# Attention scores of a hybrid block from split queries and keys: three products in the rounded format instead of products of unsplit fp32 tiles

## What is computed

```python
c_q = rms_norm(bcq, a_cq_g)
q_b = rms_norm((c_q @ a_wuq).reshape(B, S, 16, 128), a_qn_g)
k_b = rms_norm(bk.reshape(B, S, 4, 128), a_kn_g)
v_b = bv.reshape(B, S, 4, 128)
...
# for a block of 128 queries: the best 64 keys by an index score, then
sc = einsum('bqhgd,bqkhd->bqhgk', q_blk, k_g) * 128 ** -0.5
p = softmax(where(valid, sc, -inf))
out = einsum('bqhgk,bqkhd->bqhgd', p, v_g)
```

## Time and profile before

| | |
|---|---|
| median of 3 runs | 1538.51 us (1537.47 to 1538.88) |
| the profiled execution, its own time | 1538.53 us |
| its span (first to last instruction) | 1536.8 us |
| PE busy | 1532.3 us, 6996 matmuls |
| DVE busy | 994.8 us |
| ACT busy | 753.3 us |
| POOL busy | 356.7 us |
| granted TensorE clock | 1.0 of full speed over the span |

### The profile page before, as it was taken

How to read it: one execution, slowest core, us unless ns; L and a number is a source line. 1 busy time by engine, 2 the same in 40 slices (tenths; PEclk the granted TensorE clock), 3 DMA queues, 4 the chain that set the end, 5 groups by cost and what they waited for, 6 DMA issues and landing times.

```text
span 1536.8 us, 18847 instructions
## 1 busy us (share of the span) xinstructions
PE 1532.3 (100%) x6996; PEld 1271.5 (83%) x6996; DVE 994.8 (65%) x1537; ACT 753.3 (49%) x1006; POOL 356.7 (23%) x609
## 2 busy tenths in 40 slices
PE   9999999999999999999999999999999999999999
PEld 7888888888888888888878888888888888888887
DVE  6647555666769865576579667676456767664554
ACT  6745444587544444554554535534346444443332
POOL 9041212230230040126410354346200120200000
PEclk9999999999999999999999999999999999999999
DMA  9886778886787675558856787799875765666674
GB/s 291 283 240 193 223 211 232 212 234 192 231 244 209 195 221 162 161 185 273 246 182 188 225 244 217 227 276 260 251 245 178 255 213 192 210 198 194 194 247 156
DMA packets 206268, 337.77 MB, mean 220 GB/s; under 512 B 53050, under 2 KB 60521, under 8 KB 205921
## 3 DMA queue, kind: packets, MB, share of 16 engines
q1 hardware_dynamic: 184784, 288.66, 62.2%
q0 software_dynamic: 21344, 47.90, 10.9%
q10 hardware_dynamic: 48, 0.02, 0.0%
HBM read 312.81 MB, written 23.49 MB: 219 GB/s over the span
## 4 chain that ended last, share of the span: by engine, by line
PE 98%; DVE 1%; ACT 0%; issue 0%; DMA 0%; DVEq 0%
PE acc L1048 31%; PE acc L1051 31%; PE acc L1050 31%; PE mix L1111 1%; PE mix L1184 1%; PE mix L1104 0%; PE mix L1173 0%; PE mix L1019 0%; PE acc L1252 0%; DVE w_lo L1659 0%; PE mix L1170 0%; PE mix L1160 0%; ACT w_hi L1322 0%; PE mix L1158 0%; DMA xs<-in_x_dram 0%
## 5 line engine op out<-in xcount | busy, mean ns | idle before, releaser
L1659 DVE TENSOR_TENSOR w_lo<-w_raw,w_hi 128x1024 fp32r<-128x1024 f32 (+2 forms) x535 | 646.1, 1219 | 419.4 <-ACT w_hi L1322 416.2
L1322 ACT ACTIVATE w_hi<-w_raw 128x1024 fp32r<-128x1024 f32 (+2 forms) x535 | 556.2, 1050 | 526.5 <-PE acc L1051 460.1
L1048 PE MATMUL acc<-w_hi,op_hi 128*128 128x512 f32 (+1 forms) x2036 | 799.8, 393 | 0.3 <-DVE w_lo L1659 0.3
L1051 PE MATMUL acc<-w_hi,op_lo 128*128 128x512 f32 (+1 forms) x2036 | 792.5, 389 | 0.0
L1050 PE MATMUL acc<-w_lo,op_hi 128*128 128x512 f32 (+1 forms) x2036 | 792.2, 389 | 0.0
L1048 PEld LDWEIGHTS acc<-w_hi,op_hi 128*128 128x128 f32 x2036 | 382.4, 188 | 80.1 <-issue 1.3
L1051 PEld LDWEIGHTS acc<-w_hi,op_lo 128*128 128x128 f32 x2036 | 382.1, 188 | 79.9
L1050 PEld LDWEIGHTS acc<-w_lo,op_hi 128*128 128x128 f32 x2036 | 382.4, 188 | 77.8
L792 POOL DMA_DIRECT2D conv_dram<-y x48 | 30.6, 690 | 168.6 <-ACT y L1374 167.8
L792 POOL DMA_DIRECT2D y_dram<-y x32 | 20.5, 711 | 184.2 <-DVE y L2098 114.9
L946 POOL DMA_DIRECT2D bp_dram<-b_ps x48 | 31.4, 716 | 66.9 <-ACT b_ps L1543 62.8
(11 more groups left out here) (348 smaller groups left out, 974.3 us busy)
## 6 DMA issues: line engine op xcount, KB each, us to landing
w_raw<-in_w_in_dram SPq DMA_DIRECT2D x367, 512.0 KB, 4.5
w_raw<-in_w_out_dram SPq DMA_DIRECT2D x128, 512.0 KB, 4.4
w_raw<-in_w_in_dram SPq DMA_DIRECT2D x16, 384.0 KB, 3.3
w_raw<-in_a_wuq_dram SPq DMA_DIRECT2D x12, 512.0 KB, 5.9
conv_dram<-y POOLq DMA_DIRECT2D x48, 64.0 KB, 3.8
y<-conv_dram POOLq DMA_DIRECT2D x48, 64.0 KB, 4.5
w_raw<-in_a_wuqi_dram SPq DMA_DIRECT2D x6, 512.0 KB, 4.6
bp_dram<-b_ps POOLq DMA_DIRECT2D x48, 64.0 KB, 4.0
```

The costliest lines, as they stand in the source:

```text
L1048: nc.tensor.matmul(o, hi[:, kt, tok], hv[:, i, n0:n1], start=(kt == (kts if late else blk["kts"])[0]), stop=False)
L1051: last_mm = nc.tensor.matmul(o, lo[:, kt, tok], hv[:, i, n0:n1], start=False, stop=(kt == blk["kts"][-1]))
L1322: func(split_ap(w_hi, c), w_raw[:, c % RAW_BUFS, 0:n], ACT.Copy).then_inc(hi_ready, 1)
L1659: vec.tensor_tensor(split_ap(w_lo, c), w_raw[:, c % RAW_BUFS, 0:n], split_ap(w_hi, c).bitcast(F32), ALU.subtract).then_inc(lo_ready, 1)
```

## The change

The scores are no longer products of two fp32 tiles. Queries and keys are split like the big operands: ACT rounds the transposed queries to `q_hi` (two copies of 128x512 in a new piece `bqt` on ACT) and the scaled keys to `k_hi` (the second scaling writes `k_hi` instead of `b_kT`). DVE subtracts: new pieces `bql` (two subtractions of 128x512, which write `q_lo` over `b_qT`) right behind `bqt` in the same slot, and once `bkl` (128x1024, `k_lo` over `b_kT`) three slots behind `bkt`. PE makes three fp32r matmuls for each former one: `q_hi` with `k_hi`, `q_hi` with `k_lo`, `q_lo` with `k_hi`, of the same 128 or 256 columns. PE waits in `bs` for `q_lo_ready` instead of `bq_turned`. `q_hi` lies where the raw keys lay in `kv`, `k_hi` where `lane_u` lies. To have semaphores left, the ten that told of blocks brought back (`conv_moved`, `cq_moved`, `bi_moved`, `bq_moved`, `aqk_moved`) become one pair `brought`, with the counts added up in `wait_brought`; the places that wait and signal stay the same.

```diff
@@ -197,6 +197,7 @@
     at = weave(at + 9, [("bt", 0), ("bt", 1)] + [None] * 4 + [("bt", 2), ("bt", 3)])
     assert at <= end("silu", W_A + 512 * 3) + 1, (at, end("silu", W_A + 512 * 3))
     weave(at + 5, [("bkt", 0), ("yd", 12), ("yd", 13)], 2)
+    weave(at + 8, [("bkl", 0)])
     weave(end("bi", 0) + 3, [("yd", 14), ("yd", 15)], 2)
     at = weave(end("bi", 0) + 8, [("bit", 0)] + bsc_pairs(0))
     at = weave(max(at, end("bi", 1) + 10), [("bit", 1)] + bsc_pairs(1))
...
@@ -208,7 +209,7 @@
         at = end("bq", g) + (9, 2, 3, 3)[g]
         weave(at, [("bqn", g)])
         at = max(at + 9, score + 15)
-        weave(at, [("bqt", g)])
+        weave(at, [("bqt", g), ("bql", g)])
         score = at + 2
         for v in range(3):
             weave(score + 4 * v, [("bs", (g, v))])
...
@@ -285,6 +286,7 @@
         _, csq_hi, _, csq_lo = region([("y_0", [P, W_A + 1024], F32), ("csq_hi", [P, 2, 512], F32R),
                                        ("y_1", [P, D - 1024], F32), ("csq_lo", [P, 2, 512], F32R)])
         y = sb("y", [P, M, D])
+        q_hi_0, _, q_hi_1 = region([("q_hi_0", [P, 512], F32R), ("kv_0", [P, 512], F32), ("q_hi_1", [P, 512], F32R)])
         kv = sb("kv", [P, M, 1024])
         ident = sb("ident", [P, P])
         ones = sb("ones", [P, P], F32R)
...
@@ -295,6 +297,7 @@
         par = sb("par", [P, R_N + N_TAP])
         small = sb("small", [P, M, G_W])
         align(512)
+        k_hi, = region([("k_hi", [P, HKV, SEQ], F32R)])
         lane_u, lane_t = region([("lane_u", [P, BLK, LANE_C], F32), ("lane_t", [P, 320], F32)])
         rows = sb("rows", [8, 6, SEQ])
         gcol = sb("gcol", [P, 9, 8])
...
@@ -361,6 +364,9 @@
              ("b_sq", [P, 1024], F32), ("b_qT", [P, 4, SEQ], F32), ("b_kT", [P, HKV, SEQ], F32),
              ("sc", [P, 3 * P], F32), ("b_s", [P, 512], F32), ("b_ps", [P, 2, 512], F32),
              ("b_pT", [P, 2, 4, P], F32), ("top8", [P, 8], F32)])
+        _, q_lo, k_lo = region([("b_0", [P, 2 * QKT * SEQ + M * 512 + 1024], F32), ("q_lo", [P, 4, SEQ], F32R),
+                                ("k_lo", [P, HKV, SEQ], F32R)])
+        q_hi = [v[:].rearrange("p (h t) -> p h t", h=2) for v in (q_hi_0, q_hi_1)]
         b_p = b_ps[:, 0]
         bi_in = [qs[:], b_sq[:].rearrange("p (m c) -> p m c", m=M)]
         bi_T = [v.rearrange("p q (k t) -> p (q k) t", k=2) for v in bi_in]
...
@@ -455,24 +461,23 @@
-        cq_moved = [sem(f"cq_moved{i}") for i in range(2)]
+        bk_hi_ready = sem("bk_hi_ready")
+        q_hi_ready = sem("q_hi_ready")
+        q_lo_ready = sem("q_lo_ready")
-        bi_moved = [sem(f"bi_moved{i}") for i in range(2)]
-        bq_moved = [sem(f"bq_moved{i}") for i in range(2)]
-        aqk_moved = [sem(f"aqk_moved{i}") for i in range(2)]
...
@@ -586,6 +591,11 @@
 
             use = use_of[name, arg] + i
             eng.wait_ge(emptied[use % 4], use // 4 + 1)
+
+        def wait_brought(eng, kind, i):
+
+            before = {"conv": 0, "cq": 3, "bi": 4, "bq": 5, "aqk": 7}[kind]
+            eng.wait_ge(brought[i % 2], 16 * 4 * M * (before + i // 2 + 1))
 
         def wait_stored(eng, kind, arg=0):
 
...
@@ -801,7 +811,7 @@
-                bring_blocks(conv_stage(j), conv_dram[j % 2], conv_moved[j % 2])
+                bring_blocks(conv_stage(j), conv_dram[j % 2], brought[j % 2])
...
@@ -1163,15 +1173,15 @@
             def bs(arg, use):
                 g, v = arg
                 pe.wait_ge(bk_ready, 1)
-                pe.wait_ge(bq_turned, 2 * (g + 1))
+                pe.wait_ge(q_lo_ready, g + 1)
                 wait_emptied(pe, use)
+                tok, w = (slice(0, P), P) if v == 0 else (slice(P, SEQ), SEQ)
                 for i in range(4 if v == 0 else 2):
-                    if v == 0:
-                        ins = nc.tensor.matmul(bank(use)[:, i * P:i * P + P], b_qT[:, i, 0:P], b_kT[:, g, 0:P],
-                                               start=True, stop=True)
-                    else:
-                        ins = nc.tensor.matmul(bank(use)[:, i * SEQ:i * SEQ + SEQ], b_qT[:, 2 * v - 2 + i, P:SEQ],
-                                               b_kT[:, g, :], start=True, stop=True)
+                    h = i if v == 0 else 2 * v - 2 + i
+                    o = bank(use)[:, i * w:i * w + w]
+                    nc.tensor.matmul(o, q_hi[h // 2][:, h % 2, tok], k_hi[:, g, 0:w], start=True, stop=False)
+                    nc.tensor.matmul(o, q_hi[h // 2][:, h % 2, tok], k_lo[:, g, 0:w], start=False, stop=False)
+                    ins = nc.tensor.matmul(o, q_lo[:, h, tok], k_hi[:, g, 0:w], start=False, stop=True)
                 end_fill(ins, use)
 
             def bo(arg, use):
...
@@ -1520,7 +1530,13 @@
                 act.wait_ge(bk_turned, 2)
                 wait_read(act, "par", 0, 0)
                 step(func(b_kT[:], b_kT[:], ACT.Copy, scale=par[:, R_KN:R_KN + 1]))
-                func(b_kT[:], b_kT[:], ACT.Copy, scale=par[:, R_QN:R_QN + 1]).then_inc(bk_ready, 1)
+                func(k_hi[:], b_kT[:], ACT.Copy, scale=par[:, R_QN:R_QN + 1]).then_inc(bk_hi_ready, 1)
+
+            def bqt(g, use):
+                act.wait_ge(bq_turned, 2 * (g + 1))
+                for q in range(2):
+                    ins = func(q_hi[q], b_qT[:, 2 * q:2 * q + 2, :], ACT.Copy)
+                ins.then_inc(q_hi_ready, 1)
 
             def bsc(arg, use):
                 j, p = arg
...
@@ -1945,13 +1961,25 @@
                 dve.wait_ge(bk_moved, 16 * 4 * M)
                 turn_halves(two_halves(b_kT[:]), bk_turned)
 
+            def bkl(_, use):
+                dve.wait_ge(bk_hi_ready, 1)
+                vec.scalar_tensor_tensor(k_lo[:], b_kT[:], par[:, R_QN:R_QN + 1], k_hi[:].bitcast(F32), ALU.mult,
+                                         ALU.subtract).then_inc(bk_ready, 1)
+
             def bit(j, use):
-                dve.wait_ge(bi_moved[j], 16 * 4 * M)
+                wait_brought(dve, "bi", j)
                 turn_halves(bi_in[j], bi_turned)
 
             def bqt(g, use):
-                dve.wait_ge(bq_moved[g % 2], 16 * 4 * M * (g // 2 + 1))
+                wait_brought(dve, "bq", g)
                 turn_halves(two_halves(b_qT[:]), bq_turned)
+
+            def bql(g, use):
+                dve.wait_ge(q_hi_ready, g + 1)
+                for q in range(2):
+                    ins = vec.tensor_tensor(q_lo[:, 2 * q:2 * q + 2, :], b_qT[:, 2 * q:2 * q + 2, :],
+                                            q_hi[q].bitcast(F32), ALU.subtract)
+                ins.then_inc(q_lo_ready, 1)
 
             def head_norms(n, norm):
                 dve.wait_ge(b_sq_ready, M * (n + 1))
```

More of the change, by code:

```diff
@@ L408, in hybrid_kernel @@
         rows_kept = sem("rows_kept")
+        brought = [sem(f"brought{i}") for i in range(2)]
         c_rows_ready = [sem(f"c_rows_ready{i}") for i in range(2)]
@@ L419, in hybrid_kernel @@
         conv_kept = sem("conv_kept")
-        conv_moved = [sem(f"conv_moved{i}") for i in range(2)]
         conv_turned = sem("conv_turned")
@@ L916, in _ @@
                 pool.wait_ge(cq_kept, 16 * 4 * M * (i + 1))
-                bring_blocks(part, cq_dram[i], cq_moved[i])
+                bring_blocks(part, cq_dram[i], brought[i])
             pool.wait_ge(bk_norm, 2)
@@ L927, in _ @@
                 pool.wait_ge(bi_kept, 16 * 4 * M * (j + 1))
-                bring_blocks(bi_in[j], bi_dram[j], bi_moved[j])
+                bring_blocks(bi_in[j], bi_dram[j], brought[j])
             def keep_queries(g):
@@ L938, in bring_queries @@
                     wait_read(pool, "bs", (g - 1, 2))
-                bring_blocks(two_halves(b_qT[:]), bq_dram[g], bq_moved[g % 2])
+                bring_blocks(two_halves(b_qT[:]), bq_dram[g], brought[g % 2])
             def keep_shares(g, v):
@@ L968, in bring_aqk @@
                 pool.wait_ge(aqk_kept, 16 * 4 * M * (j + 1))
-                bring_blocks(two_halves((a_qT, a_kT)[j][:]), aqk_dram[j], aqk_moved[j])
+                bring_blocks(two_halves((a_qT, a_kT)[j][:]), aqk_dram[j], brought[j])
             keep_queries(0)
@@ L1577, in _ @@
             pieces = dict(evac=evac, gt=gt, g2=g2, g4=g4, gb=gb, conv=conv, csq=csq, cn=cn, ce=ce, ca=ca, cv=cv,
-                          ck=ck, cr=cr, co=co, bn=bn, bt=bt, bkn=bkn, bqn=bqn, bkt=bkt, bsc=bsc,
+                          ck=ck, cr=cr, co=co, bn=bn, bt=bt, bkn=bkn, bqn=bqn, bqt=bqt, bkt=bkt, bsc=bsc,
                           bs=bs, ae=ae, ap=ap, yt=yt)
@@ L1783, in cd @@
             def cd(i, use):
-                dve.wait_ge(conv_moved[i // 2 % 2], 16 * 4 * M * (i // 4 + 1))
+                wait_brought(dve, "conv", i // 2)
                 part = conv_stage(i // 2)[:, i % 2, :]
@@ L1928, in bt @@
             def bt(i, use):
-                dve.wait_ge(cq_moved[i // 2], 16 * 4 * M)
+                wait_brought(dve, "cq", i // 2)
                 vec.transpose(y_columns(i), y_columns(i)).then_inc(cq_turned, 1)
@@ L2060, in at @@
             def at(j, use):
-                dve.wait_ge(aqk_moved[j], 16 * 4 * M)
```

(3 more changed lines are left out.)

## The result

The changed kernel takes 1550.80 us (median of 6 runs, 1548.98 to 1558.95), the kernel before 1538.22 (6 runs, 1537.47 to 1538.88). The ratio is 1.009, with a 95% interval of 1.0068 to 1.0111. I had forecast 1541.0 and a range up to 1544.2: the direction was right, the size off by a factor of five (12.6 us between the medians instead of 2.45). The profiled execution took 1551.03 us, its span is 1549.3.

The account below looks back on a forecast made before the run. PE was taken as the bound, busy 1532.3 of 1536.8 us. Groups 0 and 1 (+0.3), group 2 (+2.0) and group 3 (+0.15) gave +2.45 us on 1538.53: 1541.0 us, range 1538.2 to 1544.2.

Parts of the forecast that it names:

- The queries: In the four `bqt` slots ACT copies twice, then DVE subtracts twice; q_lo ready 2.5 us behind the transposes.
- Products, 256 and 128 columns: Score matmuls on PE: 0.119 us each at 256 columns, 0.111 at 128; a v = 0 piece +0.44 us.
- The +0.6 in all: Score pieces on PE, all four groups: +1.76 us at 128 columns and -1.17 at 256, +0.6 together.
- The keys: One DVE subtraction in `bkl`, 1.22 us, over forty slots before the first score; costed at nothing.
- The hand-over, 2.5 us: From transposes to q_lo: ACT copies 1.13 us, DVE subtractions 1.29, two hand-overs of about 0.04 each.
- Group 2's stall of 1.65 us: Before group 2's first scores: q_lo ready at 976.2, PE there at 974.56, so PE waits 1.65 us.
- rival 1: No stall in group 2: the weight load lands 2 us earlier and q_lo is in time; 1539.1 us, chance 0.20.
- 2.0 us would have arrived in full: Group 2: DVE reaches the mask 2.0 us late, and all of it reaches PE, the 1.65 included.
- The zero slack at the split near 1010 us: DVE's split ends at 1010.39, PE starts its chunk at 1010.44; taken as the 0.3 us wait, slack zero.
- More stalls: PE also waits in group 0, or late splits reach it between groups; 1 to 2.5 us more, chance 0.10.
- The direction: Whole kernel: slower by 2.45 us, +0.16%, with under 0.2% called no change; chance of slower 0.35.

Follow-up runs that it names:

- the first experiment: Against the changed kernel, one edit: `bql` in the same slot as `bqt` instead of the next one; 1539.12 us, ratio 1.001.
- the variant with the split only where it pays: Against the changed kernel: v = 0 pieces keep one fp32 product, queries split for the last 128 tokens only, `bql` still a slot behind `bqt`; 1538.92 us, ratio 1.0008.
- the filler: Against the changed kernel: 36 extra matmuls on PE ahead of the waits for q_lo in the first score pieces, results unchanged; 1547.07 us, ratio 1.0058.

## Why the prediction was wrong

The step that failed is the opening of "The queries": that ACT copies, DVE waits for that and then subtracts, with q_lo ready "2.5 us behind the transposes". It rests on `bql` standing in the slot of `bqt`, which the description of the change says too, and which is a misreading of the code. In its place stood `bqt`, a split (and in group 1 an evacuation), `bql`: 4.6, 7.8, 4.6 and 5.1 us behind the transposes. I had listed, for each group, how much earlier than PE q_lo would be: 0.5, 2.5, -1.65 and 1.5 us. The slot in between cost 2.1, 5.3, 2.1 and 2.6 us more than the forecast 2.5, so the misreading made waits in the three groups where I had none and lengthened the fourth: 1.53, 2.76, 2.85 and 1.44 us.

Point by point:

- **Products, 256 and 128 columns:** right. 0.119 and 0.111 were forecast, 0.12 and 0.11 measured. The first product takes 0.06, which I had not looked for, but the big matmul behind the piece gives it back, so a v = 0 piece costs 0.46 more and not 0.44. The +0.6 in all was +0.3 in the medians, within their scatter.
- **The keys:** right, no wait around them.
- **The hand-over, 2.5 us:** right as a size, shown where `bql` shares the slot (2.5 us in group 2 of the first experiment).
- **Group 2's stall of 1.65 us:** the mechanism was right, the size not: 0.35 us, because the transposes, which hang on the late weight load, came 1.5 us earlier. That is most of rival 1. DVE's mask addition there starts at 977.52, 0.4 us late and not 2.0, so that 2.0 us would have arrived in full stays untested. It makes +1.2 measured instead of +2.45 for the kernel that I had in mind.
- **The zero slack at the split near 1010 us:** right, but by half a wrong reading. The split ends at 1010.39 and PE starts at 1010.44, and in the variant with the split only where it pays PE waits there. The 0.3 us wait of the earlier trace rows, which I took for this place, stands at 369.64.
- **Rivals:** "More stalls" was the right one by name and had 0.10, but its price of 1 to 2.5 us was less than a third of 8.6, and the clock, 3.4 us, was in none of my terms.
- **The direction:** it came out right, but for all except some 1.2 us by the slot and the clock, which the sum did not hold.

The sum of what happened, against the profiled execution before: 8.6 us of waits, 0.3 to 0.6 of products, and what the filler brought back, 3.7 us between medians, of which half clock explains 3.4. Together 12.6 to 12.9 us, where the profiled executions differ by 12.5 and the medians by 12.6.

## What to carry to other kernels

Where engines run the same hand-written list, place a dependent pair by what stands between the two on each engine, and read the placing function before pricing a slot: here a list within a list was worth 11.4 us of 12.6. A wait on a saturated engine can cost more than its length (2.8 us of idling and 1.7 of half clock here), and a piece that gains a step on another engine needs its slack in the plan, given together with every piece whose start hangs on another chain. Three fp32r products in place of two fp32 passes lost at 128 columns (0.46 us a piece) and won at 256 (0.14), both by little. When whole runs scatter more than the effect, compare the stretch of the trace from where the change begins.

## What the runs showed of the hardware that I had not expected

- TensorE at 2.4 GHz fell to its 1.2 GHz level after standing idle for 2.76 and 2.85 us, and the granted clock went down not in the idle time (1.00 there) but 0.7 to 1.3 us after work had begun again, and stood at 0.50 for 3.4 us. After waits of 1.53 and 1.44 us it stayed up. In two other kernels it fell behind waits of 2.31, 2.76 and 3.57 us in the same way, and behind those of 2.09 and 3.47 us already 0.1 and 0.2 us ahead of the first matmul. With the idle time filled it stayed up everywhere.
- At half clock the 128-column products start 0.21 us apart instead of 0.11, and matmuls of 512 columns 0.43 instead of 0.226: both double.
- In a row of rounded matmuls of 128 columns the first takes 0.06 us and each further one 0.11, and the matmul of 512 columns behind the row takes 0.29 instead of 0.23.
